# Four layers of mixed attention on one core: another start, another spreading of the modulation's products, and the second softmax map on ScalarE

## The reference

```
def modulate(x, g, shift, scale):
    return rms_norm(x, g) * (1 + scale) + shift

def ada_mod(cond, w, b):                       # cond: c for x, c_ctx for z; w: 1024 x 6144 a layer
    m = jax.nn.silu(cond) @ w + b
    return [a[:, None, :] for a in jnp.split(m, 6, axis=-1)]

def _diff_core(q, k, v, lam, scale):           # 8 heads, each of two softmax maps
    s = jnp.einsum('bqnd,bknd->bnqk', q, k).astype(F32) * scale
    p = jax.nn.softmax(s, axis=-1)
    p = p.reshape(b, n // 2, 2, tq, tk)
    a = p[:, :, 0] - lam * p[:, :, 1]
    return jnp.einsum('bhqk,bkhe->bqhe', a.astype(v.dtype), v)

def finish(o):
    o = rms_norm(o, subln_g) * (1.0 - lam_init)
    return o.reshape(B, o.shape[1], H * 2 * dh) @ w_o
```

## Time and profile before

| | |
|---|---|
| median of 3 runs | 2513.4 us (2512.65 to 2514.22) |
| the profiled execution | 2513.73 us, of which its span 2512.0 us |
| granted TensorE clock, mean of the span | 0.989 of full speed |
| busy: PE, ACT, DVE, POOL | 2440.7, 967.7, 1272.1, 1095.8 us |
| idle time of PE by the table of waits: for xT (L1706), h_full (L1271), w_lo (L557) | 14.0, 8.2, 11.5 us |

### The profile page before, as it was taken

One profiled execution on the slowest core, in us unless ns is written; L12 is line 12 of the kernel. 1 busy time (PEld: TensorE's weight loads), 2 busy tenths in 40 slices (PEclk: granted clock), 3 DMA queues, 4 the chain that ended last, 5 costly groups with the idle time before them and its releaser, 6 DMA issues.

```text
span 2512.0 us, 37089 instructions
## 1 busy us (share of the span) xinstructions
PE 2440.7 (97%) x12228; PEld 1990.1 (79%) x12228; DVE 1272.1 (51%) x2283; ACT 967.7 (39%) x1944; POOL 1095.8 (44%) x839
## 2 busy tenths in 40 slices
PE   8999799999999999999999999999999999998998
PEld 4566688888877777888888887778888888777998
DVE  6889876647233322236665243555765524475211
ACT  3455343332233332333323243554422324465653
POOL 0322344445434334334445443223444543434996
PEclk9999899999999999999999999999999999999999
DMA  8362345546222222235555323222555532322553
GB/s 325 118 116 78 144 172 200 196 163 226 87 94 76 70 72 91 77 101 201 195 193 186 104 83 93 76 84 93 187 187 190 192 117 81 100 84 84 185 184 133
DMA packets 117186, 341.65 MB, mean 136 GB/s; under 512 B 35568, under 2 KB 36848, under 8 KB 116336
## 3 DMA queue, kind: packets, MB, share of 16 engines
q1 hardware_dynamic: 109072, 335.01, 39.2%
q10 hardware_dynamic: 8032, 5.52, 1.4%
HBM read 335.80 MB, written 4.69 MB: 136 GB/s over the span
## 4 chain that ended last, share of the span: by engine, by line
issue 50%; PE 23%; POOL 21%; DVE 2%; ACT 1%; DMA 1%; POOLq 1%; SPq 0%; DVEq 0%; ACTq 0%
POOL w_lo L557 21%; PE low_banks L564 17%; PE high_banks L564 6%; DMA gain_f<-in_final_g 1%; PE low_banks L751 0%; DVE tmp L1747 0%; POOLq L556 0%; ACT w_hi L1160 0%; DVE dump L1676 0%; POOLq L551 0%; ACT lnm L1184 0%; DVE h_lo L1755 0%; ACT ssum_rstd L1185 0%; DVE tmp L1975 0%; DMA ada_raw<-in_ada_w 0%
## 5 line engine op out<-in xcount | busy, mean ns | idle before, releaser
L557 POOL TENSOR_TENSOR w_lo<-w_raw,w_hi 128x512 fp32r<-128x512 f32 x832 | 1095.3, 1344 | 1397.6 <-ACT w_hi L1160 1396.9
L564 PE MATMUL low_banks<-h_hi,w_hi 128*128 128x512 f32 (+1 forms) x1792 | 643.6, 359 | 14.8 <-POOL w_lo L557 7.7
L1160 ACT ACTIVATE w_hi<-w_raw 128x512 fp32r<-128x512 f32 x832 | 473.9, 624 | 420.9 <-PE low_banks L564 199.6
L564 PE MATMUL low_banks<-h_lo,w_hi 128*128 128x512 f32 (+1 forms) x1792 | 634.6, 354 | 0.0
L564 PE MATMUL low_banks<-h_hi,w_lo 128*128 128x512 f32 (+1 forms) x1792 | 634.4, 354 | 0.0
L564 PEld LDWEIGHTS low_banks<-h_hi,w_hi 128*128 128x128 f32 x1792 | 340.7, 190 | 70.8 <-issue 11.2
L1603 DVE SCALAR_TENSOR_TENSOR ssum_rstd<-ada_raw,high_banks 128x1024 f32<-128x1024 f32 x304 | 370.7, 1220 | 40.8 <-DMA ada_raw<-in_ada_w 32.5
L564 PEld LDWEIGHTS low_banks<-h_lo,w_hi 128*128 128x128 f32 x1792 | 340.7, 190 | 47.9 <-issue 1.9
L564 PEld LDWEIGHTS low_banks<-h_hi,w_lo 128*128 128x128 f32 x1792 | 340.7, 190 | 46.2
L1511 ACT ACTIVATE lnm<-low_banks 128x512 f32<-128x512 f32 (+1 forms) x88 | 47.9, 544 | 430.2 <-PE low_banks L564 430.1
L2175 DVE TENSOR_TENSOR tmp<-low_banks,lnm 128x512 f32<-128x512 f32 (+1 forms) x88 | 55.0, 625 | 290.0 <-ACT lnm L1511 286.3
(11 more groups left out here) (216 smaller groups left out, 3669.7 us busy)
## 6 DMA issues: line engine op xcount, KB each, us to landing
w_raw<-in_weights SPq DMA_DIRECT2D x424, 512.0 KB, 3.6
ada_raw<-in_ada_w SPq DMA_DIRECT2D x152, 512.0 KB, 3.8
ada_first<-in_ada_w SPq DMA_DIRECT2D x28, 512.0 KB, 7.8
ada_rest<-in_ada_w SPq DMA_DIRECT2D x12, 512.0 KB, 7.2
bias<-rpb_skew SPq DMA_DIRECT2D x64, 64.0 KB, 2.4
...
```

What stands on the lines that cost most here:

```text
L557: nc.gpsimd.tensor_tensor(out=w_lo[:, r, part], in0=w_raw[:, r, part], in1=w_hi[:, r, part], op=ALU.subtract).then_inc(lo_ready, 1)
L564: return nc.tensor.matmul(dst, lhsT, rhs, start=start, stop=stop, **kw)
L1160: nc.scalar.activation(w_hi[:, r, part], w_raw[:, r, part], ACT.Copy).then_inc(hi_ready, 1)
```

## The change

- **Start.** SP loads the condition as one row of 8 KB. PE spreads it over the partitions by multiplying it with a row of ones into four PSUM banks, and ACT's Silu reads those. Both halves of xT come next, then pair 0, bias and gains, the first two units, and the other pairs. VectorE squares row tiles 0 to 3 and adds them into one tile, ACT squares 4 to 7, and PE sums five tiles instead of eight. `constant_parts` moves behind `scaled` of m = 1, and ACT's share of it with it. WARM, the number of empty matmuls at the start, is 16 instead of 26.
- **Second map.** In `weights_` of layers 0 and 3, ACT scales the second map in place (4 or 2 Copy with a scale, behind `value_rows`), and VectorE's four (two) scalings go; each multiply-add waits for ACT's piece.
- **Products.** 4 instead of 2 stand behind the values, tile 1 has (1, 1, 1) instead of (3, 1, 1), tiles 2 to 7 have (1, 1, 2) instead of (1, 1, 1), the projection 6 instead of 12. The groups are cut anew: chunks 27 to 29, 32 to 34 and 35 to 36 load together, and slots from 20 on are columns of v_all that the finished head tiles have left (128 x 4 pieces of 1 KB); 37 to 39 come last.
- **ACT's order.** conv of the next units stands one or two h_hi earlier in the three functions named above, and the loads of layer 1's tables are issued inside `after_feed_forward`.
- **Layer 2.** Unit Q of tile 1 stands behind `scores(0)` instead of ahead of it.

```diff
-ADA_GROUPS = ((16, 0, (16, 17, 0, 4, 1, 5)), (22, 1, (2, 6, 3, 7)), (26, 0, (3,)), (27, 1, (7,)), (28, 0, (3,)),
-              (29, 1, (7,)), (30, 0, (8, 9)), (32, 1, (10, 11)), (34, 0, (12, 13, 14, 15, 16, 17)))
+ADA_GROUPS = ((16, 0, (16, 17, 0, 4, 1, 5)), (22, 1, (2, 6, 3, 7)), (26, 0, (3,)), (27, 1, (7, 20, 21)),
+              (30, 0, (3, 7)), (32, 1, (20, 21, 22)), (35, 0, (20, 23)), (37, 1, (12, 13, 14)))
 ADA_MIXER = 40
-ADA_VALUES = 2
-ADA_TILE = ((0, 1, 2), (3, 1, 1), (1, 1, 1), (1, 1, 1), (1, 1, 1), (1, 1, 1), (1, 1, 1), (1, 1, 1))
+ADA_VALUES = 4
+ADA_TILE = ((0, 1, 2), (1, 1, 1), (1, 1, 2), (1, 1, 2), (1, 1, 2), (1, 1, 2), (1, 1, 2), (1, 1, 2))
 ADA_TAIL = 8
-ADA_PROJECT = (3, 2, 2, 2, 2, 1)
-WARM = 26
+ADA_PROJECT = (1, 1, 1, 1, 1, 1)
+WARM = 16
...
+            return v_all[:, :, 2 * P * (i - 20):2 * P * (i - 20) + 2 * P]
...
-            sp.dma_start(cond_0[:, :, :], cond_in.partition_broadcast(P)).then_inc(cond_loaded, 16)
+            sp.dma_start(cond_row, cond_in.unsqueeze(0)).then_inc(cond_loaded, 16)
...
+                        last = mm(cond_wide[c][:, j, :], ones[0:1, :], cond_row[:, c, j * TOK:j * TOK + TOK], True, True)
...
                     unit(t * 2 + (n + 1), slot + 1, bank[7], H, TOK).then_inc(unit_used, 1)
...
-                    if place == 0:
-
-                        pe.wait_ge(L.qk_act, 1)
-                        unit(n + 2, slot + 2, bank[6], H, L.W).then_inc(unit_used, 1)
...
                 high(q, L, 4, 0)
+                conv(units + 3)
+                if L.kind == 1:
+                    act.dma_start(ret_rope[:, :, :], ret_rope_in).then_inc(table_in, 16)
+                    act.dma_start(ret_exp[:, :, :, :], ret_exp_in).then_inc(table_in, 16)
                 stream_square(q, 5, 1)
-                conv(units + 3)
...
+                    act.wait_ge(ratio_ready, t + (KT * L.da + 1))
+                    for qb in range(4 if L.zq else 2):
+                        x = e_x[:, qb, 1, :] if qb < 2 else e_z[:, 1, qb - 2, :]
+                        nc.scalar.activation(x, x, ACT.Copy, scale=d_st[:, 3, qb:qb + 1]).then_inc(second_scaled, 1)
...
+            def first_squares():
+
+                part = [lnm[:, :], rstd[:, :]]
+
+                dve.wait_ge(x_loaded[0], 16)
+                V.tensor_tensor(out=ssum[:, :], in0=xT[:, 0, :], in1=xT[:, 0, :], op=ALU.mult)
+                for m in range(1, KT // 2):
+                    own(V.tensor_tensor(out=part[m % 2], in0=xT[:, m, :], in1=xT[:, m, :], op=ALU.mult))
+                    last = V.tensor_tensor(out=ssum[:, :], in0=ssum[:, :], in1=part[m % 2], op=ALU.add)
...
                     first_pair(m, lambda: low_parts(m - 1))
-                    if m == 0:
-                        constant_parts()
...
+                    if m == 1:
+                        constant_parts()
...
-                            ins = V.tensor_scalar(a, x0, st[:, 2, qb:qb + 1], None, ALU.mult)
...
+                            dve.wait_ge(second_scaled, t * cols + (4 * KT * L.da + qb + 1))
+                            last = V.scalar_tensor_tensor(out=a, in0=x0, scalar=st[:, 2, qb:qb + 1], in1=x1,
                                                           op0=ALU.mult, op1=ALU.add)
```

More of the change, by code:

```diff
@@ L809, in tile_na @@
                         pe.wait_ge(L.y_lo_ready, t - 1)
-                    if place != 1:
-                        unit(t * 2 + n, slot, bank[6], H, L.W).then_inc(unit_used, 1)
+                    unit(t * 2 + n, slot, bank[6], H, L.W).then_inc(unit_used, 1)
                     if place == 0:
@@ L1251, in after_retention @@
                 conv(units + 1)
-                for m in range(3, 6):
-                    high(q, L, m, 0)
+                high(q, L, 3, 0)
+                high(q, L, 4, 0)
                 conv(units + 2)
+                high(q, L, 5, 0)
+                conv(units + 3)
                 high(q, L, 6, 0)
                 high(q, L, 7, 0)
-                conv(units + 3)
                 stream_square(q, 7, 1)
@@ L1273, in first_values @@
                         high(0, L, m, c)
+                    if m == 1:
+                        act.wait_ge(small_parts, 1)
+                        nc.scalar.activation(lam_sum[:, :, :], lam_sum[:, :, :], ACT.Exp).then_inc(small_exps, 1)
+                        act.wait_ge(small_parts, 2)
+                        own(nc.scalar.activation(lg_t[:, 1, :], lg_t[:, 0, :], ACT.Exp, scale=-1.0))
+                        nc.scalar.activation(lg_t[:, 2, :], lg_t[:, 1, :], ACT.Ln, bias=one_c[:, 0:1])\
+                            .then_inc(small_exps, 1)
                 conv(KT)
@@ L1537, in _ @@
             act.wait_ge(consts, 3)
-            for m in range(KT):
-                act.wait_ge(x_loaded[m // 4], 16)
-                if m >= 2:
-                    act.wait_ge(ssum_step[0], m - 1)
+            act.wait_ge(x_loaded[1], 16)
+            for m in range(KT // 2, KT):
+                if m >= KT // 2 + 2:
+                    act.wait_ge(ssum_step[0], m - KT // 2 - 1)
                 square(KT, m, TOK, m % 2)
@@ L1547, in _ @@
             root(0, 1)
-            act.wait_ge(lam_sums, 1)
-            nc.scalar.activation(lam_sum[:, :, :], lam_sum[:, :, :], ACT.Exp).then_inc(lam_exps, 1)
-            act.wait_ge(log_abs, 1)
-            own(nc.scalar.activation(lg_t[:, 1, :], lg_t[:, 0, :], ACT.Exp, scale=-1.0))
-            nc.scalar.activation(lg_t[:, 2, :], lg_t[:, 1, :], ACT.Ln, bias=one_c[:, 0:1]).then_inc(log_parts, 1)
             for L in plan:
@@ L2039, in attention @@
                     tile_da(1, 1)
-                    with own.loop((KT - 2) // 2, 2 * (3 + 4)) as i:
+                    with own.loop((KT - 2) // 2, 2 * (1 + 4)) as i:
                         for s in range(2):
```

116 lines of the change are left out of this document (67 added, 49 removed).

## The result

The kernel after takes 2494.6 us (median of 6 runs, 2490.8 to 2496.2), the kernel before 2513.6 (6 runs, 2510.6 to 2515.8): a ratio of 0.9923 (95% interval 0.9910 to 0.9935), faster by 19.1 us where 26.8 were forecast.

What follows compares the result with a forecast made beforehand. PE, busy 97% of the span, was taken as the bound, so gains lay in its waits and slow matmuls. Gains less costs summed to 26.8 us, from 2513.7 to 2486.9 (2486.6 in the median's frame), range 2482 to 2492.

Steps and rivals of the forecast that it cites:

- the loads decide: Rival: 1-KB pieces load at half the rate, tile 5's chunks land 5 us later, the last 3; 2495.6 us, chance 15%.
- the projection gives half: Rival: in layer 0's projection PE's wait passes to w_lo or chunks, 7 of 14.3 us arrive; 2494 us, chance 11%.
- signs for right: Trace signs expected if the forecast held, among them first value matmul near 19 and PE's xT wait under 2 us.
- Start, 8.3 forecast: Start of the kernel: scaling no longer waits for small inputs and PE's 8.20-us wait goes; gain 8.3 us (7 to 10).
- rstd by 18.4: Start: xT's second half arrives by 12.46 and rstd needs 5.9 us from there, so scaling starts at 17.9 to 18.4.
- Tile 1, 2.9 forecast: Layer 0's tile 1: two products ahead of the reciprocal go, worth 2.6 us, ACT's scalings 0.3; gain 2.9 (2 to 5).
- Tiles 2 to 7 and the group, -9.0 forecast: Layer 0: second product beside POOL costs 7.0 us (0 to 9), late chunks 27 to 29 in tile 5 cost 2 (0 to 5).
- The product waiting out a whole instruction of POOL: Rival, tiles 2 to 7: each second product takes 2.71 us, six tiles cost 10.2 instead of 7.1; 2489.7 us, chance 10%.
- Projection, 14.3 forecast: Layer 0's projection: earlier chunks and six products instead of 12 shorten PE's wait for the residual; gain 14.3 us (11 to 15.5).
- less than 1 us of amp and residual: Layer 0's projection: last item of VectorE's work, after products, residuals and sums, ending at 293 instead of 305.24.
- ACT's order, retention tables and layer 2, 9.9 forecast: Later layers: earlier conv 3.1 us, layer 1's tables loaded earlier 3.3, scores(0) a unit earlier in layer 2 3.5.
- The slower rival: Layers 0 and 3: multiply-adds wait for ACT's scalings in all 16 tiles; at 2.3 us a tile 2523 us, chance 4%.

Runs made afterwards that it cites:

- The run with the old tables: Kernel after with the product tables, chunk groups and SP's load order of the kernel before: 2494.1 us, ratio 0.9922.
- tile 4 alone: Kernel after with the second product ahead of the reciprocal instead of behind the rotation of K, only in tile 4: 2491.6 us, ratio 0.9911.
- the group moved: Kernel after with the second product ahead of the reciprocal in tiles 2 to 7 and chunks 27 to 29 issued before two loads: 2483.2 us, ratio 0.9879.
- the repeat: Kernel after measured once more, unchanged: 2492.2 us, ratio 0.992.
- the first better kernel: Kernel after with tiles 2 to 7's second product and chunks 27 to 29 earlier, WARM 8, two projection products moved to the attention's tail: 2478.6 us, ratio 0.9863.
- all six tiles moved: Kernel after with the second product ahead of the reciprocal instead of behind the rotation of K in tiles 2 to 7: 2487.8 us, ratio 0.9893.

## Why the prediction was right, and where it was not

The time lies in the range of 2476 to 2498 and on the side that had nearly all the chance, but outside the forecast's own 2482 to 2492 and 8 us above its value: 3.7 by the stages of the trace (26.8 against 23.1), 3.8 by the distance of the profiled execution from the median, the rest by the frames. That the stages miss by only 3.7 is in part luck: start, tile 1 and projection gave 7.3 less than forecast, ACT's order and the end 4.4 more. It comes out where two rivals had put it (the loads decide, 2495.6; the projection gives half, 2494), but by neither: the late group landed at 191.7, where the sum had 195.2, and the projection gave 11.2 of 14.3. Of the signs for right, three did not come: the first value matmul near 19 (21.73), PE's wait for xT under 2 us (3.46) and a wait near the start of tile 5.

- **Start, 8.3 forecast, 5.40 found.** The step that failed is "rstd by 18.4". It counted from when xT arrives, as in the earlier trace rows, and left out what stands ahead on PE and ACT: 7.1 us of spreading, 5.5 of warming, two Silu and a table load. It came at 20.4, and with the warming halved, the first value matmul came 2.1 earlier. A second step failed too, that the shift is carried to the end of the values at 0.3 for `constant_parts`: PE waits 1.14 for m = 2 (37.23), and with m paced by VectorE from there on, 5.40 of the 5.93 and of the 1.8 of faster first matmuls are left. That no wait for gain_f is left was right.
- **Tile 1, 2.9 forecast, 1.65 found.** The wait for a_z fell to 1.09, but 2.25 for kT took its place (112.73). The path from a to Q, product and K takes VectorE 6.5 us from a_z's end, while PE needs 4.2 for turn and weighted at full clock. Before, slow matmuls had covered it; I had counted them as gain. The run with the old tables has the same 2.25 behind 3.18.
- **Tiles 2 to 7 and the group, -9.0 forecast, -9.8 found**, and not for the reasons in the sum. The product's 2.27 with its read came as 2.20 (2.16 without), and a tile loses 0.84 to 0.97 instead of 1.18. But tile 4 loses 5.3: its 2.27-us wait is followed by half speed from 184.3 to 190.8, which the sum did not have, and this covered tile 5's late group, for which the sum had 2. That -9.8 is near -9.0 is luck: two errors met, and the runs with tile 4 alone, where the late group costs 3.2, and with the group moved show each. One reading was wrong as well: the 1.49-us product of before (141.53 to 143.02) lies not half but wholly in POOL's stretch; in that place after's first product took 1.93, so this one row was no measure of a half.
- **The product waiting out a whole instruction of POOL** did not come: 2.16 to 2.32, where the prediction's rival had 2.71. By the exclusive lock that the Trainium skill, "SBUF — State Buffer" ("Who interferes with whom"), states, a wait of up to a whole instruction was possible. The trace agrees that the two engines hold each other up (GpSimd's four instructions in tile 2 took 6.91 beside two products, 5.94 beside one), not that by a whole instruction.
- **Projection, 14.3 forecast, 11.2 found.** The start of the six products, 271.8, was right, though not for its reason: VectorE came to them from `subnorm` and y_lo of the last tile, at 274.68 in a trace that lies 2.72 behind the one of before at turn(7), so at 271.96 in the forecast's frame; the chunks were there. The step that failed is the end of the working, "less than 1 us of amp and residual": behind the last product came a sum of chunks of 1.10 (294.86), one more sum of squares, amp and residual, 2.56 together. All in all it took 22.7 us to 297.4 where the sum gave 21.2, and PE idled 3.46 instead of 1.7. The 1.4 for slow matmuls failed too: the clock was at 0.50 from 305 to 308 before and is from 297 to 300 after.
- **ACT's order, retention tables and layer 2, 9.9 forecast, 13.0 found** (8.62 and 4.33). The waits went in the main as said (w_lo at 677.43 in 0.17, before 1.74; no wait at 1533 for n_z, but a new one of 0.78 for kT at 1519.58). Layer 2 came as forecast, 4.3 for 4.4, with the slow transposes that I had counted there. Up to the end of layer 1 I was too low, 8.6 for 5.5, because I charged the waits alone: the slow stretches behind the 3.27 and the 2.61 (clock 0.76 over 7 us and 0.70 over 5, some 3 us) went too. The 1.3 us of the end I had not forecast. They lie behind PE's wait for h_lo (5.09 before, 5.17 after): in the 5 us from 2309 the clock before was 0.50, in those from 2287 after 0.67, and 0.66 in the repeat; no run changed them alone.
- **The slower rival**, that ACT's scalings become the tile's path, is not seen: with them back on VectorE nothing changes that can be measured.

Open stays where the 3.8 us between the profiled execution and the median of the kernel after lie. The mean granted clock, which is on record for each execution, falls as the time rises in the kernels that scatter most: 0.997 in the two executions of the first better kernel at 2476.7 and 0.995 in the two at 2480.5; 0.995 in three with all six tiles moved (to 2488.0) and 0.993 in the one at 2491.9; 0.996 down to 0.993 in order of time without warming. 0.002 of 2478 us is 5 us (2.5 to 7.4 with the rounding), so longer stretches at half speed are enough to make the scatter. In the repeat of the kernel after the order does not hold (0.994 at 2490.8, 0.995 at 2492.0), and no trace shows one of its executions near 2496.
